# A two-layer hybrid decoder on one core: cross attention's scores and values as three fp32r products instead of one fp32 product

## What is computed

```python
q = (h @ wq).reshape(b, t, X_HEADS, X_DIM)
k = (m @ wk).reshape(b, nm, X_HEADS, X_DIM)
v = (m @ wv).reshape(b, nm, X_HEADS, X_DIM)
s = jnp.einsum('bthd,bmhd->bhtm', q, k).astype(jnp.float32) * (X_DIM ** -0.5)
p = jax.nn.softmax(s, axis=-1)
o = jnp.einsum('bhtm,bmhd->bthd', p, v.astype(jnp.float32))
return o.reshape(b, t, d) @ wo
```

## Time and profile before

| | us |
|---|---|
| median of 3 runs (lowest, highest) | 2378.47 (2377.94, 2379.53) |
| the profiled execution | 2379.11 |
| its span, first to last instruction | 2377.3 |

### The profile page before, as it was taken

The page is one execution under the profiler, slowest core; times in us unless marked ns, Lnnn a source line. Parts: engine busy times, 40 slices in busy tenths (PEclk is TensorE's granted clock), DMA queues, the critical chain, the costliest instruction groups (busy, mean ns, idle before and its releaser), DMA issues.

```text
span 2377.3 us, 44376 instructions
## 1 busy us (share of the span) xinstructions
PE 2360.4 (99%) x16162; PEld 2152.6 (91%) x16162; DVE 1595.9 (67%) x3266; ACT 1318.1 (55%) x2054; POOL 1068.4 (45%) x445
## 2 busy tenths in 40 slices
PE   8999999999999999999999999999999999999999
PEld 7999889999999888888889998899999998888887
DVE  7465624879995656777674656168799945667776
ACT  5676555565555555554465665555555555555544
POOL 5757877787773000000067578777877720000000
PEclk9999999999999999999999999999999999999999
DMA  7544554456677667777664445545566776677774
GB/s 246 170 150 150 179 176 161 160 179 220 242 242 260 203 210 224 247 246 237 213 210 158 162 158 187 171 157 166 180 230 239 245 243 204 219 231 233 243 247 168
DMA packets 186851, 485.36 MB, mean 204 GB/s; under 512 B 14304, under 2 KB 81120, under 8 KB 182112
## 3 DMA queue, kind: packets, MB, share of 16 engines
q1 hardware_dynamic: 179376, 442.20, 56.5%
q10 hardware_dynamic: 7344, 41.36, 5.0%
HBM read 448.91 MB, written 34.60 MB: 203 GB/s over the span
## 4 chain that ended last, share of the span: by engine, by line
PE 98%; DVE 1%; ACT 0%; DMA 0%; POOL 0%; issue 0%; ACTq 0%; DVEq 0%
PE banks L949 29%; PE banks L514 15%; PE banks L516 15%; PE banks L515 15%; PE banks L891 5%; PE banks L550 5%; PE banks L925 3%; PE banks L892 3%; PE banks L551 2%; PE banks L854 1%; PE banks L838 1%; PE banks L819 1%; PE banks L744 0%; DMA x<-in_x 0%; PE banks L477 0%; DVE o_r L1919 0%
## 5 line engine op out<-in xcount | busy, mean ns | idle before, releaser
L445 POOL TENSOR_TENSOR w_lo<-ring,w_hi 128x1024 fp32r<-128x1024 f32 x441 | 1068.2, 2434 | 853.5 <-ACT w_hi L1003 850.5
L1003 ACT ACTIVATE w_hi<-ring 128x1024 fp32r<-128x1024 f32 x774 | 816.7, 1056 | 416.2 <-PE banks L949 339.3
L514 PE MATMUL banks<-h_r,w_hi 128*128 128x256 f32 x2464 | 701.4, 285 | 0.5 <-DVE h_r L1611 0.4
L516 PE MATMUL banks<-h_r,w_lo 128*128 128x256 f32 x2464 | 696.6, 283 | 0.0
L515 PE MATMUL banks<-h_r,w_hi 128*128 128x256 f32 x2464 | 696.4, 283 | 0.0
L949 PE MATMUL banks<-w_hi,o_r 128*128 128x512 f32 x2048 | 560.5, 390 | 0.0
L514 PEld LDWEIGHTS banks<-h_r,w_hi 128*128 128x128 f32 x2464 | 471.4, 191 | 3.4 <-issue 1.6
L515 PEld LDWEIGHTS banks<-h_r,w_hi 128*128 128x128 f32 x2464 | 471.6, 191 | 0.6 <-issue 0.5
L516 PEld LDWEIGHTS banks<-h_r,w_lo 128*128 128x128 f32 x2464 | 471.6, 191 | 0.0
L949 PEld LDWEIGHTS banks<-w_hi,o_r 128*128 128x128 f32 x2048 | 380.0, 188 | 79.3
L2093 DVE TENSOR_TENSOR w_lo<-ring,w_hi 128x1024 fp32r<-128x1024 f32 x320 | 389.6, 1218 | 31.4 <-ACT w_hi L1003 31.4
(11 more groups left out here) (332 smaller groups left out, 3123.4 us busy)
## 6 DMA issues: line engine op xcount, KB each, us to landing
ring<-in_stream SPq DMA_DIRECT2D x774, 512.0 KB, 3.4
gates_dram<-o_f ACTq DMA_DIRECT2D x32, 1024.0 KB, 5.5
o_f<-gates_dram SPq DMA_DIRECT2D x32, 1024.0 KB, 7.0
arena<-in_mem ACTq DMA_DIRECT2D x2, 1024.0 KB, 8.3
arena<-in_keys ACTq DMA_DIRECT2D x2, 1024.0 KB, 6.5
arena<-in_c_decay ACTq DMA_DIRECT2D x2, 768.0 KB, 4.8
ring<-in_stream SPq DMA_DIRECT2D x4, 256.0 KB, 6.0
x<-in_x ACTq DMA_DIRECT2D x4, 256.0 KB, 7.6
```

What stands on the lines that cost most here:

```text
L445: pool.tensor_tensor(w_lo[:, s, :], ring[:, s, :], w_hi[:, s, :], ALU.subtract).then_inc(sem(f"low{s}"), 1)
L514: pe.matmul(out, lhs[0], rhs[0], start=first, stop=False)
L516: return pe.matmul(out, lhs[1], rhs[0], start=False, stop=last)
L1003: act.activation(w_hi[:, s, :], ring[:, s, :], ACT.Copy).then_inc(sem(f"high{s}"), 1)
```

## The change

The scores and values are made of three fp32r products. For this ScalarE also writes the high part of each key and query tile (`cross_high`), after VectorE has put the sum of the two halves back into the bank (`cross_sum`), and VectorE then subtracts the high part from the bank into the low part, which now frees the bank. The values' projection and the probabilities are split by a ScalarE copy and a VectorE subtraction from the bank (`value_halves`, `value_low`, `xpt_low`). Besides:

- The first loads all go on SyncE's queue, in another order: lower-bound parameters, first half of slot 0, x0, small parameters, x2, first half of slot 1, second half of slot 0, x4, x6, second half of slot 1, slots 2 and 3, then the constants. ScalarE does a dummy Exp before it needs the first result. The first half's order on ScalarE and VectorE becomes weights of slot 0, both pairs of x, weights of slot 1.
- 11 products of zeros instead of 14.
- VectorE adds the last pair of squares too (`fold_last`), TensorE sums with one fp32 product instead of two, in both layers.
- Two weight splits of the next group stand ahead of the root at each layer's start.
- The memory's squares are made while the window's keys and values are projected, VectorE adds them up (three additions), and TensorE sums them with one fp32 product instead of eight.

```diff
+        xq_r = [part(16640, KC, T, of=arena_r), part(0, KC, T, of=arena_r)]
+        kT_r = [part(18688, KC, N_MEM, of=arena_r), part(11776, KC, N_MEM, of=arena_r)]
+        xv_r = [part(18688, NT, D, of=arena_r), part(22784, NT, D, of=arena_r)]
+        xpt_r = [part(4096, XH, 2, T, of=arena_r), part(0, XH, 2, T, of=arena_r)]
...
+            sp.dma_start(lbp, a["lb"]).then_inc(sem("lb_loaded"), 16)
+            front(0, 0)
+            load_x(0)
+            sp.dma_start(smalls[:, :, :], a["small"]).then_inc(sem("small_loaded"), 16)
+            load_x(2)
+            front(1, 0)
+            front(0, 1)
+            load_x(4)
+            load_x(6)
+            front(1, 1)
+            load(0, 2)
+            load(0, 3)
...
-            for n in range(14):
+            for n in range(11):
...
-                pe.wait_ge(sem("folded"), (l + 1) * (KC // 2 - 1))
-                for k in range(2):
-                    m = pe.matmul(bank[:, 0, 0:T], ones[:, :], square[:, k, :], start=(k == 0), stop=(k == 1))
-                m.then_inc(sem("summed"), 1)
+                pe.wait_ge(sem("folded"), (l + 1) * (KC // 2))
+                pe.matmul(bank[:, 0, 0:T], ones[:, :], square[:, 0, :], start=True, stop=True).then_inc(sem("summed"), 1)
...
-                    rms_sums(square, KC, sem("mem_squared"), 1, bank[:, 6, 0:T]).then_inc(sem("mem_summed"), 1)
+                    rms_sums(square, 1, sem("mem_folded"), 3, bank[:, 6, 0:T]).then_inc(sem("mem_summed"), 1)
...
-                            m = pe.matmul(xs[:, hd * 2 + t, :], xq[:, hd * 2 + c, t * P:(t + 1) * P],
-                                          kT[:, hd * 2 + c, :], start=(c == 0), stop=(c == 1))
+                            m = product3(xs[:, hd * 2 + t, :], [v[:, hd * 2 + c, t * P:(t + 1) * P] for v in xq_r],
+                                         [v[:, hd * 2 + c, :] for v in kT_r], c == 0, c == 1)
...
-                        m = pe.matmul(xs[:, k, :], xv[:, c, k * P:(k + 1) * P], xpt[:, k // 2, c, :],
-                                      start=(c == 0), stop=(c == 1))
+                        m = product3(xs[:, k, :], [v[:, c, k * P:(k + 1) * P] for v in xv_r],
+                                     [v[:, k // 2, c, :] for v in xpt_r], c == 0, c == 1)
...
                 split_next(-1, 3)
+                split_next(G_RQ, 0)
+                split_next(G_RQ, 1)
                 act.activation(spare[:, :], eps[:, :], ACT.Sqrt)
                 take_root(l * 3, 0)
                 for t in range(2 * SLOTS):
-                    split_next(G_RQ + t // SLOTS, t % SLOTS)
+                    if t > 1:
+                        split_next(G_RQ + t // SLOTS, t % SLOTS)
...
-                def evac_low(g, s, dst):
-
+                def evac_cross(n):
+
+                    g, s, half, k = G_XK + n // SLOTS, n % SLOTS, (kT, xq)[n // KC], n % KC
                     used(act, l * GROUPS + g, s)
-                    act.activation(dst, wide_out(s)[:, 1:2, :], ACT.Copy).then_inc(sem("low_out"), 1)
+                    act.activation(half[:, k, :], wide_out(s)[:, 1, :], ACT.Copy).then_inc(sem("low_out"), 1)
+                    ev("cross_sum", n + 1, 2 * KC)
+                    act.activation((kT_r, xq_r)[n // KC][0][:, k, :], tile_out(s), ACT.Copy).then_inc(sem("cross_high"), 1)
                     high_part(l * GROUPS + g + 1, s)
...
+                def value_halves(i):
+                    ev("token_half", P_XV + i + 1, PAIRS)
+                    act.activation(xv_r[0][:, 0, i * 512:(i + 1) * 512], bank[:, 4, :], ACT.Copy).then_inc(sem("xv_high"), 1)
+                    used(act, l * GROUPS + G_XV + i, SLOTS - 1)
+                    act.activation(xv_r[0][:, 1, i * 512:(i + 1) * 512], bank[:, 5, :], ACT.Copy).then_inc(sem("xv_high"), 1)
+                    high_part(l * GROUPS + G_XV + i + 1, SLOTS - 1)
...
+            def fold_last(l):
+
+                dve.wait_ge(sem("folded"), l * (KC // 2) + KC // 2 - 1)
+                dve.tensor_tensor(square[:, 0, :], square[:, 0, :], square[:, 1, :], ALU.add).then_inc(sem("folded"), 1)
...
+                if l == 0:
+                    dve.wait_ge(sem("mem_squared"), 1)
+                    for n in (4, 2, 1):
+                        dve.tensor_tensor(square[:, 0:n, :], square[:, 0:n, :], square[:, n:2 * n, :], ALU.add
+                                          ).then_inc(sem("mem_folded"), 1)
+                        dve.wait_ge(sem("mem_folded"), {4: 1, 2: 2, 1: 3}[n])
...
                 def add_low(n, dst):
 
+                    k = n % KC
+                    high, low = (kT_r, xq_r)[n // KC]
                     ev("low_out", n + 1, 2 * KC)
-                    k = n % KC
-                    dve.tensor_tensor(dst[:, k, :], tile_out(k), dst[:, k, :], ALU.add).then_inc(sem("bank_free"), 1)
+                    dve.tensor_tensor(tile_out(k), tile_out(k), dst[:, k, :], ALU.add).then_inc(sem("cross_sum"), 1)
+                    ev("cross_high", n + 1, 2 * KC)
+                    dve.tensor_tensor(low[:, k, :], tile_out(k), high[:, k, :], ALU.subtract).then_inc(sem("bank_free"), 1)
...
+                def value_low(i):
+                    for t in range(NT):
+                        ev("xv_high", 2 * i + t + 1, 4)
+                        cols = slice(i * 512, i * 512 + 512)
+                        dve.tensor_tensor(xv_r[1][:, t, cols], bank[:, 4 + t, :], xv_r[0][:, t, cols], ALU.subtract
+                                          ).then_inc(sem("bank_free"), 1)
+
+                value_low(0)
+                for hd in range(XH):
+                    ev("x_turned_out", hd + 1, XH)
+                    turned_p = bank[:, hd, :].rearrange("p (c t) -> p c t", c=2)
+                    dve.tensor_tensor(xpt_r[1][:, hd], turned_p, xpt_r[0][:, hd], ALU.subtract).then_inc(sem("xpt_low"), 1)
+                value_low(1)
```

More of the change, by code:

```diff
@@ L365, in load, with front, load_x @@
                              ).then_inc(sem(f"slot{s}_loaded"), 16)
-            for half in range(2):
-                for s in range(2):
-                    sp.dma_start(ring[:, s, half * 512:(half + 1) * 512],
-                                 a["stream"][s:s + 1, :, half * 512:(half + 1) * 512].rearrange("a p n -> (a p) n")
-                                 ).then_inc(sem(f"slot{s}_loaded" if half else f"front{s}_loaded"), 16)
-                    if s + half == 0:
-                        sp.dma_start(smalls[:, :, :], a["small"]).then_inc(sem("small_loaded"), 16)
+            def front(s, half):
+                cols = slice(half * 512, half * 512 + 512)
+                sp.dma_start(ring[:, s, cols], a["stream"][s:s + 1, :, cols].rearrange("a p n -> (a p) n")
+                             ).then_inc(sem(f"slot{s}_loaded" if half else f"front{s}_loaded"), 16)
+            def load_x(k):
+                sp.dma_start(x[:, k:k + 2, :], a["x"][:, k:k + 2, :]).then_inc(sem(f"x{k}_loaded"), 16)
+            sp.dma_start(lbp, a["lb"]).then_inc(sem("lb_loaded"), 16)
[10 more added lines that the diff above has]
+            load(0, 3)
             for dst, src in ((freq[:, :], a["c_freq"]), (ident[:, :], a["c_ident"]), (iota_f[:, :], a["c_iota"])):
                 sp.dma_start(dst, src).then_inc(sem("consts"), 16)
-            load(0, 2)
-            load(0, 3)
             def refill(g, s):
@@ L1011, in _ @@
                 act.sem_inc(sem(f"gates_kept{parity}"), 16)
-            act.dma_start(lbp, a["lb"]).then_inc(sem("lb_loaded"), 16)
-            for k in range(0, KC, 2):
-                act.dma_start(x[:, k:k + 2, :], a["x"][:, k:k + 2, :]).then_inc(sem(f"x{k}_loaded"), 16)
+            act.wait_ge(sem("setup_dve"), 1)
+            act.activation(spare[:, :], eps[:, :], ACT.Exp)
             act.wait_ge(sem("lb_shifted"), 1)
@@ L1039, in _ @@
                     unscaled_high(b, smalls[:, 0, 0:KC])
-                    if c == 0:
-                        half_high(1, half)
+                half_high(1, half)
             high_part(0, 2)
@@ L1141, in _ @@
                 evac_group(G_SQ, by_feature(wqk))
+                if l == 0:
+                    act.wait_ge(sem("mem_loaded"), 16)
+                    act.activation(square, mem, ACT.Square).then_inc(sem("mem_squared"), 1)
                 evac(G_SKV, 0, sv_cols.rearrange("p (a t) -> p a t", a=1))
@@ L1291, in _ @@
                     if b == 0:
-                        evac_low(G_XK, 3, by_feature(kT)(3))
+                        evac_cross(3)
                     if b == 2:
-                        evac_low(G_XK + 1, 0, by_feature(kT)(4))
+                        evac_cross(4)
                 act.dma_start(keys, a["keys"][bass.ds(l, 1)].rearrange("a p g n -> (a p) g n")
                               ).then_inc(sem("keys_loaded"), 16)
-                for s in range(1, SLOTS):
-                    evac_low(G_XK + 1, s, by_feature(kT)(SLOTS + s))
-                with act.Fori(0, 2) as i:
-                    for s in range(SLOTS):
```

(12 more changed lines are left out.)

18 lines of the change are left out of this document (9 added, 9 removed).

## The result

The changed kernel takes 2384.08 us (median of 11 runs, 2383.01 to 2386.51) against 2378.78 (11 runs) of the kernel before: ratio 1.0024 [1.0017, 1.0032]. It is 5.3 us slower; the prediction had it 3.3 us faster, at 2375.2, and its range of 2370.5 to 2379 does not hold the result. The profiled execution took 2384.08 us, its span is 2382.3 (before 2377.3).

What follows compares the result with a forecast made beforehand. TensorE, busy for 2360.4 of 2377.3 us, was taken as the bound. Gains of 4.6 (products), 2.2 (memory's sum), 1.3 and 0.8 (layer starts) less 5.6 (key-tile stalls) made 3.3 us, so 2375.2 us, range 2370.5 to 2379.

Steps and rivals of the forecast that it cites:

- Scores and values: Cross attention's score and value products: three fp32r replace one fp32; 1.16 us saved a block, 4.6 in all.
- rival C: Score and value products: an fp32r product costs 0.108 us, four blocks save 2.3 us more, 2372.9; chance 0.03.
- Halves at the key tiles: Cross attention's key tiles: halves and norm steps delay TensorE 2.8 us a layer in three waits, 5.6 in all.
- A: Key tiles: halves hidden, TensorE does not stall, gain 8.9 us, 2369.6 (2372.4 with half the stalls); chance 0.17.
- D: Key and query tiles: handovers of over 0.2 us each make every one of 32 tiles wait, 2389; chance 0.04.
- The memory's sum: Memory's sum of squares: one fp32 product for eight saves 3.0 us; 2.2 kept after an HGRN-gate wait, first layer only.
- The starts: Both layers' starts: early weight splits make low parts ready, leaving the norm's chain as limit; gains 0.8 and 1.3 us.
- The root: Norm's root at layer starts: 20.0 us in layer 1 (19.1 to 20.6); in layer 2 within 0.1 of before.
- The sum: Whole kernel: 4.6 + 2.2 + 1.3 + 0.8 - 5.6 = 3.3 us gained, giving 2375.2 us.
- E: Starts of the layers: nothing gained there, and slightly dearer waits; 2377 to 2379 us, chance 0.13.

Runs made afterwards that it cites:

- reordered: Ninth experiment: late_splits with the query norm's root behind key tile 1's high copy and one norm pair in each of key tiles 3 to 6; 2372.63 us.
- experiment 9: The run of reordered: late_splits with another order of ScalarE's and VectorE's queues at the key tiles; 2372.63 us, ratio 0.9974.
- gated: Changed kernel, except that GpSimd waits at each layer's start until VectorE has written weight slot 3's low part; 2376.50 us.
- late_splits: Changed kernel with the two early weight splits put back behind each layer's first root (a dummy Exp also writes to another tile); 2377.81 us.
- behind_root: late_splits with the weight splits of slots 0 and 1 directly behind the root, ahead of the first pair's high part; 2375.08 us.
- low3_first: Changed kernel with weight slot 3's low part ahead of the two small 128x4 operations in VectorE's queue, at both starts; 2382.08 us.
- warm: Changed kernel with 36 extra thrown-away products in the time in which TensorE waited at layer 1's start; 2383.25 us.
- early_scalars: Changed kernel with the two small 128x4 VectorE operations moved ahead of the norm's additions at each start; 2384.39 us.
- best: reordered and behind_root together in one kernel; 2369.40 us (5 runs), ratio 0.9963 to the kernel before.

## Why the prediction failed, step by step

- **Scores and values.** Forecast 1.16 us a block. Measured 6.91 - 5.74 = 1.17 for the scores of layer 1, and 3.43 - 2.27 and 6.10 - 4.95, 1.16 and 1.15, from the transposes to the end of the output tiles, which holds the values. Right, and with it the price of 0.120 us a product; rival C is out. (By the count of four passes for an fp32 product, in the Trainium skill, FP8 and Floating Point Precision, TensorE Precision Notes, it would have been 1.7, if one fp32r product took one pass's share of the time. Here it takes 0.120 us of 0.432, more than a quarter; the measurement decides.)
- **Halves at the key tiles.** Forecast 2.8 us in each layer, in three waits of 0.7, 1.6 and 0.5. Measured waits of 0.44, 1.36 and 0.31 us (tiles at 301.39, 305.80 and 309.17), in total 2.1; by the length of the whole stretch, 45.2 against 42.4 us of reordered, 2.8. Against the kernel before, layer 1 loses 3.43 - 2.24 + 1.17 = 2.4 and layer 2 6.10 - 4.04 + 1.17 = 3.2, together the 5.6 of the sum; the layers differ because the tiles of layer 1 had come more slowly before (2.83 us against 2.77). Right in size, place and cause, and experiment 9 shows the cause. Rivals A and D are out.
- **The memory's sum.** Forecast 3.0 saved and 2.2 kept, with a wait of 0.8 at the fourth hg tile. Measured: +4.36 before it, +1.35 directly behind it, so 3.0 saved, and +2.25 at the HGRN scores, so 2.1 kept. At the fourth hg tile TensorE loses 0.7 us, of which the profile shows 0.4 as a wait for ScalarE. Right.
- **The starts.** Forecast gains of 0.8 and 1.3 us; measured losses of 4.4 and 1.6. This is the step that failed: "Now these are ready early and the norm's chain is the limit." The low parts were ready early, but I counted GpSimd's work as a gain of time and not as use of a port, though its two operations for the early splits (4.65 us) moved to the moment at which VectorE's last operations ahead of the reciprocal run. I priced them at their 0.17 us; they took 2.3 each. Two things hung on it: TensorE's fourth tile wanted a low part that stood behind them, and 5.2 us of idle time brought the half clock. Of the moved steps I had weighed only what they do to ScalarE's queue. Without the block (gated) the starts come to a loss of 0.3 and a gain of 1.7, beside the forecast loss of at most 0.3 to a gain of 2 for the first and 1.3 for the second.
- **The root.** Forecast 20.0 us in layer 1 (bounds 19.1 and 20.6); it came at 20.91. The third tile's split came at 12.91 instead of 12.4, and the last early split waited 0.48 us for its weights (18.43). In layer 2 I forecast it within 0.1 us of its place; from the end of layer 1 it is 0.4 us earlier (1204.87 less 1203.03 is 1.84, layer 1 ended 2.27 later). In layer 1 this miss should cost no more than the 0.9 us by which the root came late; no run measures it alone.
- **The sum.** The terms beside the starts, as measured, make +5.6 - 4.6 - 2.1 = -1.1. With the starts as measured (+4.4 + 1.6) it gives +4.9, and the profiled executions differ by 5.0. The forecast had +5.6 - 4.6 - 2.2 - 2.1 = -3.3. None of my rivals had a mechanism at the starts that loses; E, the nearest, ended at no change.

Left open: why the first start of gated is not earlier than before. Between executions of kernels with the same beginning (late_splits, behind_root, reordered) the first root stands up to 1 us apart (18.84 and 17.81), so a term of 0.8 us there can't be told from one profiled execution each. What differs between them at the start stays open.

## What to carry to other kernels

When a step is moved to an engine's idle time, look at what else runs beside it at the new place, on the neighbours too: here a GpSimd subtraction moved ahead stopped the VectorE copy, cast, tensor-scalar or two-input operation between SBUF tiles that came beside it, for up to its whole length, and two tiny ones in a row cost the length of two of GpSimd's operations. Let such operations go first and gate GpSimd on the last of them. A small result sent to PSUM escaped the wait in the one case tried. And where a change adds handovers between two engines that both work through a list in order, write out the interleaved list: here the same steps in another order gave back 2.8 of some 3.2 us a layer.

## What was not expected of the hardware

- A 128x4 VectorE operation took 2.21 to 2.41 us instead of 0.17 when it began while GpSimd ran a 128x1024 subtraction between SBUF tiles; the same copy into PSUM took 0.17, and the reciprocal (one input) its 1.75. In the other direction GpSimd's pair took 5.67 instead of 4.7 us when a VectorE low part was waiting.
- In the first layer of the changed kernel TensorE's granted clock fell to 0.50 of full speed within a wait of 5.2 us and stayed there for some 7 us; in low3_first it fell to 0.52 after a wait of 2.7. A wait of 3.7 us in the second layer did not bring it down in the profile of the changed kernel and did in that of warm; one of 2.6 us did in early_scalars. Products in the gap kept it at 1.00.
- Query tiles, and key tiles that nothing holds up, come every 2.77 us or every 2.83 us, at a clock of 1.00: 2.83 in layer 1 and 2.77 in layer 2 of the kernel before, 2.77 among the query tiles of both layers of the changed kernel, 2.83 in both of gated. The pace can change on the way: in layer 1 of best it is 2.83 among the key tiles and 2.77 among the query tiles. Over 16 tiles this is 0.9 us, which no engine's wait explains; it limits what a comparison of one stretch in two executions can say.
